# Starting the stationary tile Ws of the PEER stages 16 bytes later in SBUF

## The reference

```
q = (hblk @ wq).reshape(PEER_BLOCK, P_HEADS, 2, D_KEY_HALF)
s = einsum('nhpd,hpkd->nhpk', q, keys)
... top 16 of each half, top 16 of their 256 sums, softmax -> gate, idx
u = u_tab[idx]
v = v_tab[idx]
act = gelu(einsum('nd,nhkd->nhk', hblk, u))
out = einsum('nhk,nhkd->nd', gate * act, v)
```

## Time and profile before

| | us |
|---|---|
| median of 3 runs | 2291.82 |
| lowest and highest of them | 2289.64, 2294.68 |
| time of the profiled execution | 2289.48 |
| its span, first to last instruction | 2288.2 |
| its TensorE busy time | 2237.6 |
| its VectorE busy time | 1868.9 |

### The profile page before, as it was taken

The page is one execution under the profiler, slowest core; times in us unless marked ns, Lnnn a source line. Parts: engine busy times, 40 slices in busy tenths (PEclk is TensorE's granted clock), DMA queues, the critical chain, the costliest instruction groups (busy, mean ns, idle before and its releaser), DMA issues.

```text
span 2288.2 us, 34776 instructions
## 1 busy us (share of the span) xinstructions
PE 2237.6 (98%) x13446; PEld 1887.6 (82%) x13446; DVE 1868.9 (82%) x3365; ACT 1199.7 (52%) x1754; POOL 168.4 (7%) x75
## 2 busy tenths in 40 slices
PE   9999999999999999999999999899999999999997
PEld 7789978777888888888888877788888888887886
DVE  8679996568688988888888888869998888887656
ACT  7555554456456555554444445455665554444553
POOL 0000000000044400000000000014430000000000
PEclk9999999999999999999999999999999999999999
DMA  8366593233555555555558996455555555556674
GB/s 293 123 207 218 192 356 114 92 120 102 184 176 185 188 175 169 172 170 175 175 175 300 340 357 235 147 185 185 185 185 173 173 171 173 175 175 217 218 239 136
DMA packets 123508, 442.32 MB, mean 193 GB/s; under 512 B 13760, under 2 KB 16832, under 8 KB 122704
## 3 DMA queue, kind: packets, MB, share of 16 engines
q1 hardware_dynamic: 117464, 425.04, 56.4%
q10 hardware_dynamic: 5880, 15.06, 1.9%
HBM read 436.88 MB, written 3.16 MB: 192 GB/s over the span
## 4 chain that ended last, share of the span: by engine, by line
PE 82%; DVE 10%; ACT 3%; DMA 2%; issue 2%; SPq 0%; ACTq 0%; DVEq 0%
PE psum L442 21%; PE psum L450 13%; PE psum L452 13%; PE psum L451 13%; PE psum L443 10%; PE psum L445 3%; PE psum L2864 3%; DVE low L2600 3%; DVE acc L1777 2%; PE psum L444 1%; DVE cv L2108 1%; DMA ring<-in_peer_v 1%; ACT spl L1097 1%; ACT cv L1398 1%; PE psum L918 1%
## 5 line engine op out<-in xcount | busy, mean ns | idle before, releaser
L2600 DVE TENSOR_TENSOR low<-ring,spl 128x1024 fp32r<-128x1024 f32 x638 | 779.2, 1228 | 255.0 <-ACT spl L1097 253.4
L1097 ACT ACTIVATE spl<-ring 128x1024 fp32r<-128x1024 f32 x702 | 735.4, 1053 | 288.2 <-DMA ring<-in_peer_u 163.7
L442 PE MATMUL psum<-hT,spl 128*128 128x512 f32 x2016 | 730.7, 401 | 2.5 <-DVE hT L1757 2.5
L443 PE MATMUL psum<-hT,low 128*128 128x256 f32 x2016 | 566.5, 281 | 0.0
L442 PEld LDWEIGHTS psum<-hT,spl 128*128 128x128 f32 x2016 | 381.2, 189 | 81.2 <-issue 3.1
L450 PE MATMUL psum<-spl,Ws 128*128 128x512 f32 x1024 | 407.0, 398 | 7.0 <-DVE Ws L2638 7.0
L452 PE MATMUL psum<-spl,Ws 128*128 128x512 f32 x1024 | 399.6, 390 | 0.0
L451 PE MATMUL psum<-low,Ws 128*128 128x512 f32 x1024 | 398.3, 389 | 0.0
L443 PEld LDWEIGHTS psum<-hT,low 128*128 128x128 f32 x2016 | 382.8, 190 | 9.6
L1706 ACT ACTIVATE Ws<-S 128x256 fp32r<-128x256 f32 x256 | 106.6, 417 | 357.0 <-PE psum L452 352.4
L2921 POOL TENSOR_TENSOR low<-ring,spl 128x1024 fp32r<-128x1024 f32 x64 | 162.0, 2532 | 1135.6 <-ACT spl L1097 1135.6
(11 more groups left out here) (413 smaller groups left out, 3038.1 us busy)
## 6 DMA issues: line engine op xcount, KB each, us to landing
ring<-in_peer_u SPq DMA_DIRECT2D x256, 512.0 KB, 3.5
ring<-in_peer_v SPq DMA_DIRECT2D x256, 512.0 KB, 3.7
vring<-in_ada_w SPq DMA_DIRECT2D x56, 512.0 KB, 6.2
ring<-in_w_up SPq DMA_DIRECT2D x44, 512.0 KB, 5.2
aring<-in_ada_w SPq DMA_DIRECT2D x40, 512.0 KB, 5.2
ring<-in_ab_in SPq DMA_DIRECT2D x32, 512.0 KB, 3.5
ring<-in_peer_wq SPq DMA_DIRECT2D x32, 512.0 KB, 4.3
ring<-in_w_down SPq DMA_DIRECT2D x22, 512.0 KB, 5.9
```

Of the source, the lines that this page charges most:

```text
L442: q.matmul(b[:, :].rearrange("p (z t) -> p z t", z=2), l[0], r, start=start, stop=False)
L443: return q.matmul(b[:, 0:256], l[1], r[:, 0], start=False, stop=False)
L1097: q.activation(P.spl[:, m % SLOTS, 0:w], P.ring[:, m % SLOTS, 0:w], ACT.Copy).then_inc(*P.hi.mark(m))
L2600: q.tensor_tensor(P.low[:, n % SLOTS, 0:w], P.ring[:, n % SLOTS, 0:w], P.spl[:, n % SLOTS, 0:w].bitcast(F32), ALU.subtract).then_inc(*P.lo ...
```

## The change

`Ws` is allocated 1,540 words wide at the same place and used from its fifth word on, so each of its three buffers starts 16 bytes later (byte 221,840, which is 16 past a multiple of 64). `Eb`, which begins where `Ws` ended, moves 8 words (byte 228,000, which is 32 past a multiple of 64). Shapes, strides, instructions, their order and their waits are the same.

```diff
-        self.Eb = a("Eb", 36352, [128, 8, 64], F16)
-        self.Ws = a("Ws", 34816, [128, 3, 2, 256], F32R)
+        self.Eb = a("Eb", 36360, [128, 8, 64], F16)
+        self.Ws = a("Ws", 34816, [128, 1540], F32R)[:, 4:1540].rearrange("p (j z t) -> p j z t", j=3, z=2)
```

## The result

The changed kernel takes 2301.85 us, the kernel before 2290.59 us (medians of 14 runs each). The ratio is 1.0049, with a 95% interval of 1.0042 to 1.0057: slower by half a per cent, 11.3 us. The forecast was 2292 us within 2287 to 2298, with 9% for slower.

What follows compares the result with a forecast made beforehand. TensorE, busy in 98% of the span, was taken to bound the kernel. Loads, array, ScalarE, VectorE and Eb each added 0, so the profiled 2289.5 us stays; the forecast median was 2292 us, range 2287 to 2298.

Steps and rivals of the forecast that it cites:

- What can be touched: Only Ws's loads, matmuls, ScalarE copies and VectorE subtractions, plus VectorE's writes and reads of Eb, can change in time.
- The load and its slack: Ws weight loads take 188 ns against a 226.7 ns matmul pace; slack 39 ns or at least 107; cost 0.
- The load rival: Ws loads grow past their slack; doubled to 376 ns they give 2750 us, or about 2333 by rate; chance 2%.
- The array's fixed part: In TensorE's pace, 13.4 ns per matmul beyond 512 columns' 213.3 ns, perhaps taken by the load; its change taken as 0.
- the one comparison of starts: Loads from `mixed`, 32 bytes past a multiple of 64, and `hn`, at a multiple, both take 140 ns at the median.
- Slower, by the array's fixed part: Ws loads take twice as many turns from the moving stream: +13.4 ns for 3,072 matmuls, 41 us, 2333 us; chance 7%.
- The faster rival: Stationary and moving rows, moved 16 bytes apart, miss each other in memory: up to -41 us, 2251 us; chance 3%.
- ScalarE, VectorE, `Eb`: ScalarE's copy, VectorE's subtraction and the operations on Eb keep their durations at the new starts; cost 0 each.
- the two fixed parts of 217 ns: VectorE durations of 1278 and 481 ns less 1.04 ns a word, used to show a start off by a word costs nothing.

Runs made afterwards that it cites:

- e5_ws64: Kernel before with Ws alone starting 64 bytes later and Eb following it; 2305.82 us, ratio 1.0069.
- e9_base64: Kernel before with every SBUF tile starting 64 bytes later, all distances between tiles kept; 2291.30 us, ratio 1.0003.
- e4_base16: Kernel before with every SBUF tile starting 16 bytes later, all distances between tiles kept; 2291.12 us, ratio 1.0016.
- e1_eb32: Kernel before with only Eb moved, 32 bytes later, Ws unchanged; 2291.24 us, ratio 1.0000.
- e13_wsstay: The change, but from j = 3 on ScalarE and VectorE write their results over S instead of into Ws; 2298.86 us in one execution.

## Why the prediction was wrong, point by point

- **What can be touched.** Right: the difference is in the 3,072 `Ws` matmuls, and no other stretch between stages took 1 us more; the u stages only changed places.
- **The load and its slack.** Right in kind: loads stayed at 188 to 192 ns and never reached the pace. The load rival had no part.
- **The array's fixed part.** This is the step that failed: "I take 0, since the one comparison of starts shows none". The 13.4 ns over 512 columns became 20.0 (233.3 - 213.3). The comparison was of the wrong thing twice over. The earlier trace rows compare the durations of loads in a transpose, while the price sits in the distance from matmul to matmul and leaves the durations of loads almost alone (188 to 192 ns). And they compare two starts, while what counts among multiples of 64 is how far the stationary rows stand from the moving ones (e5_ws64 against e9_base64); each offset of `Ws` alone from 4 to 128 bytes cost 3.9 ns or more. A 32-byte start is no nearer to a 16-byte one than 64 bytes are: all three cost 6.7 to 6.9 ns when `Ws` takes them alone.
- **The rival that came true.** "Slower, by the array's fixed part" had its place and its lower bound right (anything from 1.5 ns a matmul shows) but its mechanism wrong in part: no doubling, and no need of a start in the middle of 32 or 64 bytes, since 64 bytes cost as much. That such a start counts as well isn't excluded: e4_base16 is slow with all distances kept. It had 7%. Its sum, 41 us, was off by the factor of a half in the pace (6.7 for 13.4 ns) and by another 0.6 from tiles that were slow already, tiles that stayed short, and waits that took up the rest.
- **The faster rival** held that stationary and moving rows, all at the same place modulo 64, meet each other and would gain by being moved apart. For `Ws` the opposite holds: the common place (with 256, its equal) is the best of the eleven tried. For `hT` as the moving operand of two blocks a gain came, 3 ns a pair in the first 64 tiles of a layer, but that it comes from moving the two apart isn't shown (e4_base16 gained without it).
- **ScalarE, VectorE, `Eb`.** Right: 418, 417, 415 and 417 ns, and e1_eb32 measured the `Eb` part at 1.0000. The working had one soft place: the two fixed parts of 217 ns are equal by construction, since the rate comes from the same two durations; what carries is that this rate, 1.04 ns a word, is that of other lines.
- **Rule against trace.** The Trainium skill's page "SBUF — State Buffer", section on specifications, gives 16-byte lines as the unit, and by it I saw no cost. The pace after contradicts its use here: 64 bytes cost as much as 16. The Trainium skill's page "TensorE: Matmul & The Clock Gate", section "Step-by-step: what each phase is for", says that loading the next tile's weights takes no read bandwidth from the running matmul. This trace doesn't agree: with loads of 188 to 192 ns the pace is 226.6 to 234.4 ns by where the stationary rows stand relative to the moving ones. What in the chip couples the two isn't shown.

## What to carry to other kernels

Where TensorE streams back to back with a load for each matmul, the addresses of its operands are a parameter: look at the pace from start to start (not at durations), and keep stationary and moving tiles of float32 words at equal places modulo 256 bytes and at multiples of 64 (equal places 16 bytes past one were slow in the v stage), or sweep the offset if the moving operand has more than one block. A view inside an allocation does it without another instruction. When a change moves a tile, compare the distances to its partners in the matmul before and after, for every tile behind it in the layout too: 64 bytes between `Ws` and its moving rows cost 0.5 to 0.7% here. When a gain is claimed, compare the same stage in several executions of unchanged kernels first: a u stage differed by 2.4 us with nothing changed in it. And when a trace has a fixed part that nothing explains, as the 13.4 ns, it is the place to put the chance, not the place for a zero.

## What the runs showed of the hardware

- The pace of matmuls with a load each (float32 rounded to fp32r, 512 moving columns, granted clock 1.00) is a repeating pattern into which the row falls, with means of 226.7, 230 and 233.3 ns and some between. The same addresses gave 226.7 and 233.3 in one execution (the change, e13_wsstay), or 230.1, 231.1 and 233.3 (e4_base16). The pattern changes at breaks.
- With the moving rows in place, it depends on how far the stationary rows stand from them: 226.6 and 226.7 ns at 0 and 256 bytes, 228.3 to 234.4 at the nine offsets between; 4 bytes are enough to lose 5.9 ns. Among multiples of 64 it is the distance alone (e5_ws64, e9_base64). With all operands 16 bytes past a multiple of 64 distance 0 gave 230 to 233 ns (e4_base16).
- The pairs of the u stage have two patterns as well: with the same addresses the last 64 tiles took 347.4 or 352.7 ns a pair, in either layer.
- After a break the kernel before needs up to a tile of twelve matmuls to reach its short pattern: 2.84 us for the first twelve, 2.72 afterwards.
- Durations hardly show it. The loads kept 188 to 192 ns, the matmuls' median went from 389 to 394, and the distance between starts by 6.7.
